# Router logits from the raw residual sum with the layer norm folded in, normalisation on ScalarE, first gather in fp32

## The reference, cut to what matters

```python
x = _layernorm(DEEPNORM_ALPHA * x + mix, ln1_g, ln1_b)
...
logits = jnp.dot(x2d.astype(f32), router_w.astype(f32)) + router_b.astype(f32)
top_val, top_idx = lax.top_k(logits, TOP_K)          # 4 of 32 experts
top_w = jax.nn.softmax(top_val, axis=-1)
...
hgu = xb @ moe_w_gu[e] + moe_b_gu[e]                 # xb: the tokens of expert e
act = (up + 1.0) * gate * jax.nn.sigmoid(SWIGLU_ALPHA * gate)
return act @ moe_w_down[e] + moe_b_down[e]
...
x = _layernorm(DEEPNORM_ALPHA * x + ffn, ln2_g, ln2_b)
```

## Time and profile before

| | |
|---|---|
| median of 3 runs | 1298.52 us (1295.99 to 1301.59) |
| profiled execution | 1293.87 us, its span 1292.1 us |
| PE busy | 1149.3 us (89%) |
| DVE, ACT, POOL busy | 397.4, 277.1, 36.8 us |
| DMA | 457.73 MB, 354 GB/s over the span |

### The profile page before, as it was taken

The page is one execution under the profiler, slowest core; times in us unless marked ns, Lnnn a source line. Parts: engine busy times, 40 slices in busy tenths (PEclk is TensorE's granted clock), DMA queues, the critical chain, the costliest instruction groups (busy, mean ns, idle before and its releaser), DMA issues.

```text
span 1292.1 us, 18129 instructions
## 1 busy us (share of the span) xinstructions
PE 1149.3 (89%) x7027; PEld 605.9 (47%) x7027; DVE 397.4 (31%) x700; ACT 277.1 (21%) x425; POOL 36.8 (3%) x50
## 2 busy tenths in 40 slices
PE   6999999986899998989898888989898989898895
PEld 5998878873443443333333333334333333333341
DVE  4788477758202122020202020211202020202025
ACT  5685444434110111111010101011111101010101
POOL 1000020005000000000000000000000000000000
PEclk9999999995999999999999999999999999999998
DMA  9545476538899999999999999999999999999992
GB/s 283 180 131 176 152 239 236 203 122 336 319 419 417 418 418 418 418 418 418 418 418 418 417 417 417 417 417 418 418 418 418 418 418 418 418 418 416 415 416 99
DMA packets 118388, 457.73 MB, mean 354 GB/s; under 512 B 10376, under 2 KB 49304, under 8 KB 85232
## 3 DMA queue, kind: packets, MB, share of 16 engines
q1 hardware_dynamic: 113984, 445.52, 86.7%
q0 software_dynamic: 3152, 11.31, 2.5%
q10 hardware_dynamic: 1216, 0.42, 0.1%
HBM read 451.25 MB, written 5.95 MB: 354 GB/s over the span
## 4 chain that ended last, share of the span: by engine, by line
PE 43%; DMA 24%; SPq 22%; DVE 5%; issue 3%; ACT 2%; DVEq 0%; ACTq 0%
DMA gu_w<-in_moe_w_gu 24%; PE pool L529 16%; SPq L403 12%; PE pool L777 10%; SPq L399 10%; PE pool L810 6%; PE ub L740 5%; ACT arena L1052 1%; PE pool L803 1%; PE ob L789 1%; PE pool L538 1%; ACT wh L843 1%; DMA low_w<-in_w_in 1%; PE ub L789 1%; DVE wl L1089 1%
## 5 line engine op out<-in xcount | busy, mean ns | idle before, releaser
L777 PE MATMUL pool<-gu_w,arena 128*64 128x512 f32 x2048 | 465.9, 597 | 42.9 <-DMA gu_w<-in_moe_w_gu 42.6
L777 PEld LDWEIGHTS pool<-gu_w,arena 128*64 128x64 f32 x2048 | 139.8, 136 | 350.8 <-issue 208.9
L1487 DVE TENSOR_SCALAR arena<-pool 128x512 f32<-128x512 f32 x32 | 22.1, 692 | 765.8 <-PE pool L777 765.8
L810 PE MATMUL pool<-dn_w,arena 128*64 128x512 f32 x1024 | 226.8, 595 | 21.6 <-ACT arena L1052 21.6
L529 PE MATMUL pool<-xh,wh 128*128 128x264 f32 x576 | 166.6, 289 | 6.4 <-DVE xl_most L1082 5.5
L529 PE MATMUL pool<-xh,wl 128*128 128x264 f32 x576 | 163.7, 284 | 0.0
L810 PEld LDWEIGHTS pool<-dn_w,arena 128*64 128x64 f32 x1024 | 70.7, 137 | 157.1 <-issue 127.9
L529 PE MATMUL pool<-xl_most,wh 128*128 128x264 f32 x504 | 143.6, 285 | 0.0
L1050 ACT ACTIVATE arena<-arena 128x512 f32<-128x512 f32 x32 | 20.2, 631 | 491.9 <-DVE arena L1487 491.9
L529 PEld LDWEIGHTS pool<-xh,wh 128*128 128x128 f32 x576 | 109.2, 190 | 13.0 <-issue 10.3
L529 PEld LDWEIGHTS pool<-xh,wl 128*128 128x128 f32 x576 | 108.7, 189 | 0.0
(11 more groups left out here) (282 smaller groups left out, 720.7 us busy)
## 6 DMA issues: line engine op xcount, KB each, us to landing
gu_w<-in_moe_w_gu SPq DMA_DIRECT2D x256, 1024.0 KB, 19.9
dn_w<-in_moe_w_down SPq DMA_DIRECT2D x256, 512.0 KB, 20.8
dn_w<-in_w_in SPq DMA_DIRECT2D x24, 1024.0 KB, 5.4
dn_w<-in_w_branch SPq DMA_DIRECT2D x8, 1024.0 KB, 5.5
gu_w<-in_state_gla POOLq DMA_DIRECT2D x8, 512.0 KB, 6.7
out_gla_sample<-gu_w POOLq DMA_DIRECT2D x8, 512.0 KB, 6.7
dn_w<-in_w_o SPq DMA_DIRECT2D x4, 1024.0 KB, 5.3
arena<-in_xT SPq DMA_DIRECT2D x2, 1056.0 KB, 6.2
```

The source lines that it names most:

```text
L777: last = mm(out, xg[:, k, j * CAP:(j + 1) * CAP], gu_w[:, k, cols], start=False, stop=(k == NB - 1))
L810: last = mm(DOWN[s * CAP:(s + 1) * CAP, :], act_t[:, k % 4, k // 4 * CAP:(k // 4 + 1) * CAP], dn_w[:, k, s * HF:(s + 1) * HF], start=(k == ...
L1487: ts(gbuf, GATE, LIMIT, None, ALU.min).then_inc(gclip, 1)
```

## The change

1. Logits from yT, not from the normalised rows: with w' = router_w * ln1_g, the logits are rs * (yT . w') - rs * mean * sum(w') + sum(router_w * ln1_b) + router_b. VectorE makes w' and the sums during the mixer (seven operations after job sc). TensorE sums them over the partitions with one matmul, job cd, between m7 and m8.
2. The product yT . w' is made in halves, blocks 0 to 3 after wo5 (ahead of yt00 and wo6), blocks 4 to 7 after wo7. The four blocks of a half go to four groups of 32 partitions; a 128 x 32 matrix of stacked identities, `stack`, sums the groups while it turns them to token order (job lg).
3. Statistics come straight from the PSUM banks of yt, those of the first half after the residual sum of wo5. Memsets and two casts move between the w_o blocks.
4. ScalarE normalises: ytok * rs + nmr. The normalised rows carry neither gain nor bias. They come in with the evictions: of xt into yacc (with ALPHA), and of the gather into xg.
5. Only xt0 to xt2 stand ahead of the rank counts (job rk), xt3 to xt7 behind.
6. The first gather reads the fp32 rows with an fp32 pick matrix `pick0`: 24 matmuls. ScalarE evicts the first four blocks, VectorE the others. The bf16 parts are made after it, by ScalarE and VectorE; GpSimd has no part in it any more. The loops on VectorE begin after `xp_lo`.
7. In the loop, ScalarE evicts a gather in eight instructions (`take`) in place of one.
8. The loads of ln1_g and ln1_b as rows are gone.

```diff
-    jobs += [f"m{n}" for n in range(2 * NB)] + [f"b1{n}" for n in range(NB)]
+    jobs += [f"m{n}" for n in range(NB)] + ["cd"] + [f"m{n}" for n in range(NB, 2 * NB)] + [f"b1{n}" for n in range(NB)]
...
-    jobs += [f"xt{n}" for n in range(4)] + [f"xt{n}" for n in range(4, NB)] + ["lg", "rk"]
+    jobs += ["lg"] + [f"xt{n}" for n in range(3)] + ["rk"] + [f"xt{n}" for n in range(3, NB)]
...
-            pool.dma_start(ln1[:, 0, :], ln1_g.partition_broadcast(P).rearrange("p a e -> p (a e)")).then_inc(ln_in, 16)
-            pool.dma_start(ln1[:, 1, :], ln1_b.partition_broadcast(P).rearrange("p a e -> p (a e)")).then_inc(ln_in, 16)
...
-                if t == 2:
-                    pool.wait_ge(xp_hi, 2)
-                    g.tensor_tensor(y, x1[0:rows, t, :], xparts[t][0][0:rows, :], ALU.subtract).then_inc(xp_r1_small, 1)
-                else:
-                    pool.wait_ge(xp_r2, i)
-                pool.wait_ge(xp_mid, i + 1)
-                g.tensor_tensor(y, y, xparts[t][1][0:rows, :], ALU.subtract).then_inc(xp_r2, 1)
...
+            pe.wait_ge(cdw_done, 3)
+            open_job(pe, "cd")
+            mm(bank("cd")[:, 0:2 * E], ones[:, :], cdw[:, :], start=True, stop=True).then_inc(fl("cd"), 1)
...
+            def logits(half):
+
+                for k in range(4 * half, 4 * half + 4):
+                    wait_drained(pe, f"wo{k}")
+                for j in range(4):
+                    k = 4 * half + j
+                    last = mm(ob[32 * j:32 * j + E, 0, 0:T], router_w[:, k, :], yT[:, k, :], start=(half == 0),
+                              stop=(half == 1), skip_group_check=True)
+                return last
...
+            def turn_x(blocks_):
+
+                for n in blocks_:
+                    name = f"xt{n}"
+                    turn(name, [(bank(name)[:, first:first + rows], ytok[0:rows, t, n * P:(n + 1) * P])
+                                for t, (first, rows) in enumerate(TILES)])
+
+            for n in range(6):
+                project(f"wo{n}", 3)
+            logits(0)
+            turn_y(0)
+            for n in range(6, NB):
+                project(f"wo{n}", 3)
+            wait_filled(pe, "wo7")
+            pe.wait_ge(od_full, DEC)
+            pe.sem_inc(gu_used, NB)
+            pe.sem_inc(dn_used, NB)
+            logits(1).then_inc(lgt_full, 1)
+            turn_y(1)
+            pe.wait_ge(lgt_read, 1)
+            open_job(pe, "lg")
+            for t, (first, rows) in enumerate(TILES):
+                last = mm(bank("lg")[0:rows, t * E:(t + 1) * E], lgs[:, first:first + rows], stack[:, :],
+                          start=True, stop=True)
+            last.then_inc(fl("lg"), 1)
             pe.wait_ge(y_norm, NT)
-
-            def logits(k):
-                wait_drained(pe, f"xt{k}")
-                return mm(ob[0:E, 0, 0:T], router_w[:, k, :], x1T[:, k, :], start=(k == 0), stop=(k == NB - 1))
-
-            for n in range(NB):
-                name = f"xt{n}"
-                turn(name, [(bank(name)[:, first:first + rows], ytok[0:rows, t, n * P:(n + 1) * P])
-                            for t, (first, rows) in enumerate(TILES)])
-                if n >= 3:
-                    logits(n - 3)
-            for k in range(NB - 3, NB):
-                last = logits(k)
-            last.then_inc(lgt_full, 1)
-            pe.wait_ge(lgt_read, 1)
-            turn("lg", [(bank("lg")[0:rows, t * E:(t + 1) * E], lgT[:, first:first + rows])
-                        for t, (first, rows) in enumerate(TILES)])
+            turn_x(range(3))
...
+            turn_x(range(3, NB))
+            pe.wait_ge(pick0_done, 1)
+            for half in range(2):
+                for t, (first, rows) in ((2, TILES[2]), (0, TILES[0]), (1, TILES[1])):
+                    for c in range(4):
+                        n = 4 * half + c
+                        last = mm(GATH[:, half, c * P:(c + 1) * P], ytok[0:rows, t, n * P:(n + 1) * P], pick0[0:rows, t, :],
+                                  start=(t == 2 and c == 0), stop=(t == 1), skip_group_check=True)
+                last.then_inc(gath0, 1)
+            pe.wait_ge(gath0, 2)
+            pe.sem_inc(gath_done, 1)
...
+                pe.wait_ge(xp_lo, NT)
...
-            pe.wait_ge(xp_lo, NT)
-            pe.wait_ge(picked, 1)
-            gather()
-            wait_drained(pe, "rk")
+            for n in range(4, NB):
+                wait_drained(pe, f"xt{n}")
+            pe.wait_ge(xg0_dve, 1)
...
+                if s == 1:
+                    sc.wait_ge(lgt_full, 1)
+                    nc.scalar.copy(lgs, ob[:, 0, 0:T]).then_inc(lgt_read, 1)
...
-                    wait_filled(sc, name)
+                    sc.wait_ge(y_stat, NT * s + t + 1)
...
+            sc.wait_ge(y_rs, 1)
+            for n in range(NB):
+                wait_drained(sc, f"yt{n % NT}1")
+            for t, (first, rows) in enumerate(TILES):
+                a(ytok[0:rows, t, :], ytok[0:rows, t, :], ACT.Identity, bias=nmr[0:rows, t:t + 1],
+                  scale=rs1[0:rows, 1, t:t + 1]).then_inc(y_norm, 1)
+            for n in range(NB):
+                wait_filled(sc, f"xt{n}")
+                a(yacc[:, n, :], bank(f"xt{n}")[:, 0:T], ACT.Identity, bias=affine[:, NB + n:NB + n + 1],
+                  scale=affine[:, n:n + 1]).then_inc(dr(f"xt{n}"), 1)
+
+            def take(n, view):
+
+                return a(xg[:, n, :], view, ACT.Identity, bias=con("ln1_b")[:, n:n + 1], scale=con("ln1_g")[:, n:n + 1])
+
+            sc.wait_ge(gath0, 1)
+            for n in range(4):
+                last = take(n, GATH[:, 0, n * P:(n + 1) * P])
+            last.then_inc(xg_ready, 1)
...
+            for part, ready, made in ((1, xp_r1, xp_mid), (2, xp_r2, xp_lo)):
+                for t in (0, 1, 2):
+                    rows = TILES[t][1]
+                    sc.wait_ge(ready, t + 1)
+                    nc.scalar.copy(xparts[t][part][0:rows, :], ytok[0:rows, t, :]).then_inc(made, 1)
...
-                        nc.scalar.copy(xg, GATH[:, :, :].rearrange("p a n -> p (a n)").rearrange("p (n c) -> p n c", n=NB)
-                                       ).then_inc(xg_ready, 1)
+                        for b in range(NB):
+                            last = take(b, GATH[:, b // 4, b % 4 * P:(b % 4 + 1) * P])
+                        last.then_inc(xg_ready, 1)
...
+            me.done(tt(rw_b, router_w, con("ln1_b").unsqueeze(2).to_broadcast([P, NB, E]), ALU.mult))
+            V.reduce_sum(stack[:, :], ident[:, :].rearrange("p (g e) -> p e g", g=4), AX_X).then_inc(cdw_done, 1)
+            me.settle()
+            V.reduce_sum(cdw[:, E:2 * E], rw_b.rearrange("p k e -> p e k"), AX_X).then_inc(cdw_done, 1)
+            me.done(tt(router_w, router_w, con("ln1_g").unsqueeze(2).to_broadcast([P, NB, E]), ALU.mult))
+            me.done(ts(affine[:, 0:NB], con("ln1_g"), ALPHA, None, ALU.mult))
+            me.done(ts(affine[:, NB:2 * NB], con("ln1_b"), ALPHA, None, ALU.mult))
+            me.settle()
+            V.reduce_sum(cdw[:, 0:E], router_w.rearrange("p k e -> p e k"), AX_X).then_inc(cdw_done, 1)
...
+                if b == 0:
+                    wait_filled(v, "cd")
+                    v.wait_ge(rb_in, 16)
+                    me.done(V.tensor_copy(cdv[:, 0:E], bank("cd")[:, 0:E]))
+                    tt(cdv[:, E:2 * E], bank("cd")[:, E:2 * E], rb[:, :], ALU.add).then_inc(dr("cd"), 1)
...
+                if n == 0:
+                    me.done(V.memset(mv1[:, :, :], 1.0))
+                    me.done(V.tensor_copy(before16[:, :], before[:, :]))
+                    me.done(V.tensor_copy(ones16[:, :], ones[:, :]))
+                if n == 2:
+                    for t in (sel, sel16, ex):
+                        me.done(V.memset(t[:, :, :], 0.0))
+                    me.done(V.memset(keep3[:, :], 1.0))
+                    me.settle()
+                    me.done(V.memset(keep3[:, 0:NT * E:E], 0.0))
+                if n in (1, 3, 4):
+                    V.memset(xparts[2][(1, 3, 4).index(n)], 0.0).then_inc(xp_zero, 1)
+                if n in (5, NB - 1):
+                    s = n // 7
+                    for t, (first, rows) in enumerate(TILES):
+                        wait_filled(v, f"yt{t}{s}")
+                        V.bn_stats(st1[0:rows, t, s, :], bank(f"yt{t}{s}")[0:rows, :]).then_inc(y_stat, 1)
...
-                ts(ytok[0:rows, t, :], ytok[0:rows, t, :], mv1[0:rows, t, 0:1], rs1[0:rows, 1, t:t + 1],
-                   ALU.subtract, ALU.mult).then_inc(y_norm, 1)
...
+            stt(nmr[:, :], mv1[:, :, 0], -1.0, rs1[:, 1, :], ALU.mult, ALU.mult).then_inc(y_rs, 1)
...
+            for t, (first, rows) in enumerate(TILES):
+                last = stt(lg[0:rows, t, :], bank("lg")[0:rows, t * E:(t + 1) * E], rs1[0:rows, 1, t:t + 1],
+                           cdv[0:rows, E:2 * E], ALU.mult, ALU.add)
...
+                me.done(stt(lg[0:rows, t, :], cdv[0:rows, 0:E], nmr[0:rows, t:t + 1], lg[0:rows, t, :], ALU.mult, ALU.add))
...
```

(21 more changed lines are left out.)

130 lines of the change are left out of this document (29 added, 101 removed).

## The result

The changed kernel takes 1288.71 us in the median of 9 runs (1283.66 to 1291.63), the kernel before 1296.47 us in the 9 runs it is compared with (1293.91 to 1301.59). The ratio is 0.9918, with a 95% interval of 0.9901 to 0.9934: about 10.6 us faster (8.6 to 12.8); the plain difference of the two medians is 7.8 us. The forecast was 12.8 us less, 1285.7 us, so the time lies in its range and 3 us above its likeliest value. The forecast was counted from a median of 1298.52 us for the kernel before, 2 us above the 1296.47 here. The profiled execution took 1287.14 us with a span of 1285.2.

A forecast was written before the change was run, and what follows sets the result against it. The expert weight stream was taken as the bound, stalled once by the router's chain. -12.1 (gap) - 1.6 (dip) + 0.6 (logits) + 0.3 (cd) = -12.8 us, so 1285.7 us in the median, range 1279 to 1293.

The forecast's parts named there:

- The bound and the cap: Expert weight stream at memory rate is the bound; of 15.6 us cut from the router's chain, 12.1 count.
- the gap and the dip: Weight stream's 28 GB/s stretch at 317 to 330 us, 12.1 us lost, and 352 GB/s at 345 to 355, 1.6 lost.
- The margin: First expert forecast at 309.5 us, 4.8 us before 314.3, the latest start at which the weight stream never stops.
- rival 1: Router's chain shortened by less than the cap needs: 3.0 us of standstill stay, -8.9 us, 1289.6 us; chance 0.20.
- Top 4: Router's choice of experts: max starts at 291.3 us; two operations on 96 elements take 0.3 each without GpSimd, saving 3.5.
- Transposes and gather: Ahead of the first expert: transposes 0.84 us a block; fp32 gather 8.3 us, 18 instructions at lower clock, 12.3 at worst.
- logits(0), fold and cd: Work ahead of the stream: first logits half 0.6 us (to 1.5), fold nothing (to 2.6), cd 0.3 (0 to 0.8).
- Splits behind the gather: bf16 splits on ScalarE and VectorE from 309 to about 319 us, with 4.6 us of cover before VectorE's loop work.
- Loop evictions: ScalarE's eight evictions per gather in the expert loop, 4.6 us at most beside 7.09 of w_down matmuls: cost nothing.
- rival 4: Slower: the loop's eight evictions lie on TensorE's path, 1.6 us lost in each of 15 pairs, 1309.7 us; chance 0.04.
- Rival 3: Nothing moves, as an unseen wait holds the first expert at 325 us: 1298.5 us; chance 0.05.
- Rival 2: Work ahead of the stream is dearer (fold, cd, w_o memsets, logits(0)), 5.4 us: -8.3 us, 1290.2 us; chance 0.06.

The follow-up runs named there:

- hold_short: The changed kernel with five idle matmuls of 256 columns between the first gather's eviction and the first expert; median 1289.78 us, ratio 0.9928 to the kernel before.
- hold_long: The changed kernel with nineteen idle matmuls of 256 columns between the first gather's eviction and the first expert; median 1294.72 us, ratio 0.9962 to the kernel before.
- again: The changed kernel run once more with nothing edited; median 1288.85 us, ratio 0.9924 to the kernel before.
- logits_late: The changed kernel with the first half of the logits moved behind wo7, ahead of the second half; median 1288.25 us, ratio 0.9927 to the kernel before.
- warm: The changed kernel with idle fp32 matmuls on TensorE ahead of four pauses in the mixer; median 1289.15 us, ratio 0.9935 to the kernel before.
- best: logits_late plus the idle matmuls of warm without those ahead of b00, and 30 idle ones ahead of the transposes; median 1284.94 us, ratio 0.9906 to the kernel before.
- pool_busy: The changed kernel with four unused GpSimd additions of 128 x 1024 elements beside the top 4; median 1294.12 us, ratio 0.9970 to the kernel before.
- one_copy: The changed kernel with one plain copy for the loop's eight evictions, without gain and bias for experts from 2 on; median 1289.06 us, ratio 0.9929 to the kernel before.

## Why the prediction was right, step by step

The changed trace is put on the prediction's clock by the stream's start: the forecast is 284.42 + 0.6 = 285.0, so 4.9 us are taken off.

- **The bound and the cap.** Right. A chain that got 15.05 us shorter, counted from the stream's start (forecast: 40.73 less 309.5 - 285.0, so 16.2), gained the gap and the dip, 13.7 us forecast; measured are 14.7 in the pair of traces and 13.2 in the mean of the three of before (911.4 less 898.2). hold_short and hold_long show it by putting the gap back.
- **The margin.** Mis-sized. The prediction let TensorE start up to 29.3 us after the stream's start (314.3 less 285.0) without a gap, which with its 2.5 us is a reload at 31.8. The gap's corner is at 30.5 to 31.1, about 1 us earlier: the buffers ran full at 32.6, as forecast, so the term that was too small is the "0.8 for the first data, an estimate", which should have been near 1.6. The 2.5 held wherever the clock was up (2.51 in again, logits_late, warm and best); in the changed kernel's trace the first w_gu block ran partly at 1.2 GHz, and it was 3.40. With the chain 1.2 us later than forecast too, the margin of 4.8 us shrank to about 1.9. The dip has a loss of its own, which the prediction priced at 1.6 us and did not count into the margin. So rival 1 was nearer than the margin of 4.8 made it look.
- **Statistics and normalisation.** Right: on the old clock statistics end at 288.5 (forecast 288.6), scale and shift 289.7 (289.9), normalisation 293.3 (293.0 to 293.9).
- **Top 4.** Right: MAX8 at 290.9 (291.3), the pick 296.8 to 297.3 (296.6 to 297.2), scan and add 0.36 and 0.26 us for 0.3 each. The reason given, GpSimd, was right too. Rival 1 priced a top 4 as slow as before at 2.0 us for the rank counts. pool_busy is a harder case, with GpSimd busy through the whole choice, and shows 5.06; its expectation had it at 3.5 for the choice and 1 for the first expert, which was too little.
- **Transposes and gather.** Right, size and working. 8.58 us for 8.3, at 1.2 GHz to about 310, which took in 22 of the 48 instructions where the forecast had 18. In the traces the instructions follow each other 0.112 us apart at 2.4 GHz and 0.213 at 1.2. The gather took 11.47 us in hold_short, all at 1.2 GHz (12.3 forecast). No run had it at 2.4 GHz throughout: some 6.1 us is an estimate from the three, with (11.47 - 8.58) / 26 = 0.11 us saved for each instruction, and the forecast had 6.2. By the Trainium skill (TensorE: Matmul & The Clock Gate, "Part 4: PE-mode transpose") transposes don't raise the clock; the trace agrees, with the granted clock (third column from the right) at 0.50 through the transposes and until 310 us. The last two lines are hold_short's gather and the clock inside it:

```profile
298.00:300.00 2.00, 1.77 (x7) 1.07 (x8) 0.72 (x6) 0.77 (x3) 0.00 (x0) 0.50 1.03 426
...
308.00:310.00 2.00, 2.00 (x11) 2.00 (x11) 0.00 (x0) 0.00 (x0) 0.00 (x0) 0.50 1.05 430
310.00:312.00 2.00, 2.00 (x16) 1.76 (x15) 0.00 (x0) 1.49 (x5) 0.00 (x0) 0.98 0.98 406
...
304.64 11.47 PE L738 MATMUL ub<-arena 8*128 8x128 f32 x48
306.00:310.00 4.00, 4.00 (x20) 3.77 (x18) 0.00 (x0) 0.00 (x0) 0.00 (x0) 0.50 1.01 416
```

  In best, where the clock was up ahead of them, it stayed up through the transposes and fell at 303 us, 1 us behind their end.
- **Evictions of the first gather.** VectorE's four took 1.37 us, not 0.8, and TensorE followed 0.65 us later: the first expert at 310.7 on the old clock, for 309.5.
- **logits(0), fold and cd.** 0.7 for 0.6 and 0.28 for 0.3. The fourfold speedup that the Trainium skill gives as the most (TensorEngine Tiling, "Theoretical Speedup") would have made the half 0.4 by the prediction's estimate; it took 0.58, close to the 0.62 of the row.
- **Splits behind the gather.** Hidden: ScalarE ends them at 324.2, TensorE the first w_gu block at 331.6.
- **Loop evictions.** Hidden, 2.91 us for "4.6 at most"; rival 4 falls with one_copy.
- **What the sum lacked.** The exit pause, some 0.3 us, and whatever else delays the stream. By its own list the prediction would be wrong "if the stream starts over 1.5 us later": it started 5.5 us later in this trace, and 3.1 in the means of the traces. Only 1.0 us of that is traced to the added work (0.7 for the logits, 0.3 for fold and cd, forecast 0.6 and 0.3). With the mean stream of before the traced terms give -13.2 + 0.7 + 0.3 + 0.3 = -11.9, inside the measured 8.6 to 12.8 less; with all of the 3.1 it would be -9.8, inside too. Which is nearer, the runs don't tell. So the gain was right by its mechanism, and the side of the costs agrees only within the scatter of the start. The profiled difference of 6.9 us is smaller because the first trace of before had no fall of the clock that delayed the stream. Rival 3 falls: the first expert started early. Rival 2 falls as it was put, since the added work cost 1.0 us, not 5.4.

## What to carry to other kernels

Where a stream of loads is the bound, cut the span at the stream's start, its last wait and the end, in every trace. The stream's own length repeats to 0.5 us among traces without a gap, where medians have runs spread over 8 us; the steps of one engine's operations ahead of it told costs of 0.3 us. A chain ahead of such a stream is worth shortening until the next load goes out before the buffers are full, with 1.6 us for its data here; leave a margin of some microseconds there, since the clock alone moved the first reload by 1 us and the gather by 3, and stop. Before a cost is charged to a change because one trace of the old kernel lacks it, take a second trace of the old kernel.
